# Overflowing pairs of experts: nested branches with one common Else, and gate and up loads issued ahead of down loads

## The reference

```python
def hierarchical_moe(h, wg_r, bg_r, we_r, be_r, w_gate, w_up, w_down):
    hf = h.reshape(n, d_)                                   # 512 x 1024
    gsel = jnp.argmax(group_logits, axis=-1)                # one group of 8 experts per token
    top_val, top_idx = lax.top_k(in_group, TOP_K_IN_GROUP)  # two experts in it
    gates = gp * jax.nn.softmax(top_val, axis=-1)
    ...
    def expert_block(args):
        tok, e = args
        xb = h_pad[tok]
        hid = jax.nn.silu(xb @ w_gate[e]) * (xb @ w_up[e])  # 1024 -> 256
        return hid @ w_down[e]                              # 256 -> 1024
    ...
    y = jnp.zeros((n + 1, d_), h.dtype).at[buf_tok].add(out)[:n]
```

## Time and profile before

| | us |
|---|---|
| runs of the kernel | 2876.44 median of 3 (2875.86 to 2879.05) |
| the profiled execution | 2879.38, its span 2877.6 |
| PE busy | 2341.8 (81%) |
| PE weight loads busy | 1718.4 (60%) |
| DVE busy | 1195.9 (42%) |
| ACT busy | 855.9 (30%) |
| POOL busy | 190.1 (7%) |
| DMA | 377.27 MB, mean 131 GB/s |
| granted TensorE clock, mean | 0.856 |

### The profile page before, as it was taken

The page is one execution under the profiler, slowest core; times in us unless marked ns, Lnnn a source line. Parts: engine busy times, 40 slices in busy tenths (PEclk is TensorE's granted clock), DMA queues, the critical chain, the costliest instruction groups (busy, mean ns, idle before and its releaser), DMA issues. The chain is left out here.

```text
span 2877.6 us, 32597 instructions
## 1 busy us (share of the span) xinstructions
PE 2341.8 (81%) x13804; PEld 1718.4 (60%) x13804; DVE 1195.9 (42%) x1868; ACT 855.9 (30%) x1270; POOL 190.1 (7%) x190
## 2 busy tenths in 40 slices
PE   7889999958953677679999979866698688887874
PEld 5768888837722676368888768555696533333331
DVE  3346664374168444556664344344424411111112
ACT  4324442274241222434442243553103210110000
POOL 0000000000014000000000000000310011111100
PEclk9889999979976677789999989955857699998997
DMA  4112222222200100112222213300103379999986
GB/s 180 59 59 88 90 101 91 85 88 88 73 0 9 15 13 13 74 59 93 98 98 90 105 64 112 95 0 8 17 1 144 124 320 419 418 418 413 402 347 271
DMA packets 106598, 377.27 MB, mean 131 GB/s; under 512 B 54960, under 2 KB 55744, under 8 KB 67536
## 3 DMA queue, kind: packets, MB, share of 16 engines
q1 hardware_dynamic: 94064, 363.55, 33.5%
q0 software_dynamic: 12384, 11.58, 1.4%
HBM read 375.31 MB, written 27.53 MB: 140 GB/s over the span
## 5 line engine op out<-in xcount | busy, mean ns | idle before, releaser
L579 PE MATMUL ps<-xh,wh 128*128 128x512 f32 x1384 | 552.7, 399 | 86.2 <-DVE wl L546 35.0
L580 PE MATMUL ps<-xl,wh 128*128 128x512 f32 x1384 | 548.5, 396 | 0.0
L581 PE MATMUL ps<-xh,wl 128*128 128x512 f32 x1384 | 547.5, 396 | 0.0
L546 DVE TENSOR_TENSOR wl<-raw,wh 128x2048 fp32r<-128x2048 f32 (+2 forms) x127 | 264.5, 2082 | 326.7 <-ACT wh L540 326.7
L579 PEld LDWEIGHTS ps<-xh,wh 128*128 128x128 f32 x1384 | 266.0, 192 | 160.4 <-issue 55.3
L581 PEld LDWEIGHTS ps<-xh,wl 128*128 128x128 f32 x1384 | 265.7, 192 | 56.5
L580 PEld LDWEIGHTS ps<-xl,wh 128*128 128x128 f32 x1384 | 266.4, 193 | 54.7
L2955 PE MATMUL ps<-egu,XT 128*64 128x512 f32 x1088 | 245.9, 605 | 28.6 <-DMA egu<-e_up 27.7
L540 ACT ACTIVATE wh<-raw 128x2048 fp32r<-128x2048 f32 (+2 forms) x127 | 220.4, 1735 | 82.4 <-PE ps L864 69.2
L3007 PE MATMUL ps<-ed,HID 128*64 128x512 f32 x544 | 151.3, 706 | 63.4 <-DMA ed<-e_down 61.6
L2955 PEld LDWEIGHTS ps<-egu,XT 128*64 128x64 f32 x1088 | 83.5, 139 | 166.6 <-issue 142.4
(11 more groups left out here) (460 smaller groups left out, 3487.1 us busy)
## 6 DMA issues: line engine op xcount, KB each, us to landing
egu<-e_gate SPq DMA_DIRECT2D x68, 1024.0 KB, 14.8
egu<-e_up SPq DMA_DIRECT2D x68, 1024.0 KB, 25.1
ed<-e_down SPq DMA_DIRECT2D x68, 1024.0 KB, 24.7
raw<-up SPq DMA_DIRECT2D x44, 1024.0 KB, 4.8
raw<-down SPq DMA_DIRECT2D x32, 704.0 KB, 4.0
raw<-rwkv_rkv SPq DMA_DIRECT2D x12, 1024.0 KB, 4.8
raw<-in_dn SPq DMA_DIRECT2D x8, 1024.0 KB, 4.8
raw<-sgu_u SPq DMA_DIRECT2D x4, 1024.0 KB, 8.3
```

What stands on the lines that cost most here:

```text
L546: e.tensor_tensor(K.WL[s][:, 0:n], K.RAW[r][:, 0:n], K.WH[s][:, 0:n].bitcast(F32), SUB).then_inc(*K.w_low.mark(i))
L579: e.matmul(o, h[:, q, k], x_high[:, k], start=k == 0, stop=False)
L580: e.matmul(o, h[:, q, k], x_low[:, k], start=False, stop=False)
L581: last = e.matmul(o, l[:, q, k], x_high[:, k], start=False, stop=k == KT - 1)
```

## The change

The eight branches, which stood one behind another, stand inside each other: the body of level q contains the If of level q+1, so an engine leaves all further levels with one branch. The Else of level q adds at once what all levels from q to 39 would have added, after waits for its engine's own semaphores; the waits for all engines in the Else of SP and POOL are gone. On SP a level issues gate and up of its own pair, and then the down loads of the pair before (`downs(q - 1)`); the down loads of the last executed pair stand in the Else that ends the levels (`last(q - 1, True)`), and SP then waits there until they have landed. The bodies of PE, ACT, DVE and POOL are as before.

```diff
         e.dma_start(K.EGU[slot][:, half], src).then_inc(*K.egu_in[slot].landing(i, half))
 
 
-def load_down(K, e, i, index=None):
+def load_down(K, e, i, index=None, counted=True):
+
     slot = i % 4
     w = K.A["e_down"]
     if i < 64:
@@ -2877,7 +2878,8 @@
         src = None if index is None else w[bass.ds(index, 1)].rearrange("a (p j) n -> p (a j) n", p=128)
     if i >= 4:
         e.wait_ge(*K.expert_sum("down", (i - 4) // 2))
-    e.dma_start(K.ED[slot][:, :, :], src).then_inc(*K.ed_in[slot].landing(i))
+    e.dma_start(K.ED[slot][:, :, :], src).then_inc(*(K.ed_in[slot].landing(i) if counted else (K.ed_in[slot].sem, 16)))
+    return K.ed_in[slot]
...
-def over_the_count(K, e, engine, q, body):
-
-
-    K.board.point(engine, "over", q)
+def over_the_counts(K, e, engine, body, last=None):
+
+
+
     if not e.real:
-        K.skipped[engine, q] = owed(K, engine, body)
+        for q in range(32, NP):
+            K.board.point(engine, "over", q)
+            K.skipped[engine, q] = owed(K, engine, lambda: body(q))
+        if last:
+            K.skipped[engine, NP] = owed(K, engine, lambda: last(NP - 1))
         return
-    met = dict(e.met)
-    with e.real.If(K.regs[engine] > 2 * (q - 32)):
-        body()
-    e.met = met
-    with e.real.Else():
-        for s, first, by in K.skipped[engine, q]:
-            e.real.wait_ge(s.sem, first)
-        if engine in ("POOL", "SP"):
-            for t in K.board.all_at("over", q):
-                e.real.wait_ge(*t)
-        for s, first, by in K.skipped[engine, q]:
-            e.real.sem_inc(s.sem, by)
+
+    def level(q):
+        met = dict(e.met)
+        with e.real.If(K.regs[engine] > 2 * (q - 32)):
+            body(q)
+            if q + 1 < NP:
+                level(q + 1)
+            elif last:
+                last(q)
+        e.met = dict(met)
+        with e.real.Else():
+            added = {}
+            for p in range(q, NP + 1):
+                for s, first, by in K.skipped.get((engine, p), ()):
+                    n = added.setdefault(s, [first, 0])
+                    n[1] += by
+            if last and q > 32:
+                for s in last(q - 1, True):
+                    added[s][0] += 16
+                    added[s][1] -= 16
+            for s, (first, by) in added.items():
+                e.real.wait_ge(s.sem, first)
+            for s, (first, by) in added.items():
+                if by:
+                    e.real.sem_inc(s.sem, by)
+        e.met = met
+
+    level(32)
...
-    for q in range(32, NP):
-        def body():
-            for i in (2 * q, 2 * q + 1):
-                if e.real:
-                    K.index[i] = e.real.value_load(K.OVI[0:1, i - 64:i - 63], min_val=0, max_val=63)
-                load_gate_up(K, e, i, K.index.get(i))
-            for i in (2 * q, 2 * q + 1):
-                load_down(K, e, i, K.index.get(i))
-        over_the_count(K, e, "SP", q, body)
+
+    def downs(q, again=False):
+        return [load_down(K, e, i, K.index.get(i), not again) for i in (2 * q, 2 * q + 1)]
+
+    def body(q):
+        for i in (2 * q, 2 * q + 1):
+            if e.real:
+                K.index[i] = e.real.value_load(K.OVI[0:1, i - 64:i - 63], min_val=0, max_val=63)
+            load_gate_up(K, e, i, K.index.get(i))
+        if q > 32:
+            downs(q - 1)
+    over_the_counts(K, e, "SP", body, downs)
...
-    for q in range(32, NP):
-        def body():
-            turn_pe(K, e, q)
-            gate_up_pe(K, e, q)
-            turn_hidden_pe(K, e, q)
-            down_pe(K, e, q)
-        over_the_count(K, e, "PE", q, body)
+
+    def body(q):
+        turn_pe(K, e, q)
+        gate_up_pe(K, e, q)
+        turn_hidden_pe(K, e, q)
+        down_pe(K, e, q)
+    over_the_counts(K, e, "PE", body)
```

More of the change, by code:

```diff
@@ L3143, in experts_act, with body @@
     overflow_count(K, e, "ACT")
[L3144 to L3149, removed]
+    def body(q):
+        turn_act(K, e, q)
+        gate_up_act(K, e, q)
+        down_act(K, e, q)
+    over_the_counts(K, e, "ACT", body)
     K.board.point("ACT", "mixed")
@@ L3166, in experts_dve, with body @@
     overflow_count(K, e, "DVE")
[L3167 to L3173, removed]
+    def body(q):
+        turn_dve(K, e, q)
+        gate_up_dve(K, e, q)
+        turn_hidden_dve(K, e, q)
+        down_dve(K, e, q)
+    over_the_counts(K, e, "DVE", body)
     K.board.point("DVE", "mixed")
@@ L3197, in experts_pool, with body @@
     overflow_count(K, e, "POOL")
[L3198 to L3207, removed]
+    def body(q):
+        gather(K, e, q + 1)
+        if q + 1 < NP:
+            e.wait_ge(*K.xg_more(q + 1))
+            e.memset(K.MARK[:, 0, q:q + 1], 0.0).then_inc(*K.pool_expert.mark("gathered", q + 1))
+        scatter(K, e, q, True)
+        e.wait_ge(*K.otok_more(q))
+        e.memset(K.MARK[:, 1, q:q + 1], 0.0).then_inc(*K.pool_expert.mark("scattered", q))
+    over_the_counts(K, e, "POOL", body)
     K.board.point("POOL", "mixed")
```

## The result

The changed kernel takes 2882.1 us (median of 20 runs, 2880.16 to 2883.62), the kernel before 2877.68 (20 runs, 2875.63 to 2880.14): a ratio of 1.0015, 95% interval 1.0008 to 1.0022, or 4.4 us more (by the interval 2.3 to 6.3). That is inside the 0.2% that I had called no change, on the slow side and clear of nothing, and as large as the predicted sum of 4.4.

A forecast was written before the change was run, and what follows sets the result against it. Full, in-order DMA queues bound the expert stage, then a 4.02 us tail before `OT`. Terms 5.7 + 2.0 - 3.3 = +4.4 us on a median of 2876.44 gave 2880.8 us, range 2876.0 to 2884.3.

The forecast's parts named there:

- Down loads late: Pair 32's down loads, queued behind four gate and up loads, make PE start its down product at 2836.9: cost 5.7 us.
- Rival 2: Pair 32's down loads aren't late; PE starts that down product at 2831.23 as before: -3.3 us, 2873.1, chance 0.10.
- Clock: PE idles 6.2 us before pair 32's down product, so its clock is lowered there: cost 2.0 us, between 0 and 3.65.
- Rival 3: PE's clock after its idle time isn't lowered, or recovers at once: +2.4 us, 2878.8, chance 0.12.
- Block 67's up comes too early to be of use: Block 67's up lands 5 us earlier, but gate and up of pair 33 can't use it: gain 0.
- Common Else: At the end, `OT` goes out 0.7 us behind the last MEMSET instead of 4.02: gain 3.3 us.
- lower bound of 2.0: Least gain at the kernel's end, if SP's last waits take as long again as the rest: 2.0 us.
- Far branches: PE's single jump past six pairs takes 2.9 us after its last product, hidden with 2.0 us to spare.
- Rival 1: POOL's far jump over six levels stalls on the path as PE's did, costing 2.9: +7.3 us, 2883.7, chance 0.13.
- SP's repeated down loads: Pair 33's down loads now stand in SP's Else, which SP reaches before 2812.27: cost 0.
- Sum: All terms after the 32 fixed pairs together: +4.4 us, to 2880.8 us, 0.15% slower.
- anything ahead of 2800 us: Sign of being wrong: the change should leave everything before about 2800 us as it was.

The follow-up runs named there:

- last experiment: Six matmuls added in PE's idle time ahead of gate and up of pair 32, against the kernel with common Else and old load order: 2874.23 us, ratio 0.9987.
- third experiment: Changed kernel plus seven matmuls whose result nothing reads, in PE's idle time before the down product of pair 32: 2880.08 us, ratio 1.0006.
- the second: Changed kernel, but down loads of pair 32 moved behind two loads instead of four (between gate and up of blocks 66 and 67): 2875.85 us, ratio 0.9993.
- fourth experiment: Changed kernel with gate and up of blocks 64 and 65 also put ahead of the down loads of pair 31: 2879.88 us, ratio 1.0005.

## Why the prediction was right, step by step

- **Down loads late (5.7 us): right.** By the rows PE's wait grew from 0.52 to 6.31, 5.8. It started at 2835.91, a microsecond before the forecast, behind a gate and up that itself had started 1.6 earlier. The run with the old order has no such wait, that with half the move 0.45 of it: the loads land in the order of issue, and the slack is what decides. Rival 2 falls with that.
- **Clock (2.0 us, taken from a nearby row): 2.4** (6.03 against 3.65), shown by the run in which PE is kept busy. Rival 3 falls. Gate and up of pair 32 took 0.48 more than before too (9.60, 9.12), in a lowered clock as before; I had no term for it, and it is not the change's, since the run with the old order has 9.43.
- **Block 67's up comes too early to be of use: right**, gate and up of pair 33 wait for `XT`. (Four loads of 2.8 behind 2820.04 give 2831.2, not the 2831.8 that I wrote; nothing hung on it.) The last experiment shows the other side of it: in the old order that load is one step from being the limit.
- **Common Else (3.3 us): 3.84**, 4.02 down to 0.18. I had left 0.3 for SP's last waits; they were nearly all done before POOL's addition. What I had put at nothing is the 0.3 us that the way from the last product to the MEMSET got longer, so 3.5 in all. My lower bound of 2.0 does not come out of my own numbers (4.02 less twice 0.7 is 2.6).
- **Far branches: right that they are hidden, wrong on where PE's stands.** I charged 2.9 from the end of PE's last product on. It took 3.766, but it overlapped with the last down product, so its addition stood at 2856.8, 5 us ahead of POOL's. POOL's single jump took no longer than 0.050. Rival 1 falls. By the Trainium skill (Runtime: NRT & Kernel Launch, "Instruction fetch mechanics") a branch beyond the pages held waits for a fetch; PE's 3.766 agrees in kind, and POOL's jump over six levels, which passes far less code, shows no stall.
- **SP's repeated down loads: right.** The down loads of pairs 32 and 33 are all out by 2815.25 (2808.36 + 6.89), and the last down product waits 0.52 for DVE and for no load.
- **Sum.** The three forecast terms measure 5.8 + 2.4 - 3.8 = 4.4; with the 0.3 us ahead of the MEMSET and 0.1 less in the turning of pair 33 it is 8.56 - 0.48 - 3.52 = 4.6 by the rows, 4.4 by the medians. The mechanism was right in each part, but that the sum met the tenth is luck: the clock was put 0.4 too low and the gain up to 0.5 too low, and the two cancel; and the interval of the ratio is 2 us wide to each side. The profiled spans differ by 3.7 (2881.3, 2877.6): in the changed kernel's profile block 65's up landed sooner after its issue, and PE waited 4.37 for it instead of 6.73. That isn't the change's doing: the same order of loads shows 6.50 in the third experiment's trace.
- **Did anything ahead of 2800 us move?** I had named that as a sign of being wrong, and in the profiled execution something did. The down product of pair 29, first in the kernel before, then in the changed one:

```profile
2792.12 3.65 PE L3007 MATMUL ps<-ed,HID 128*64 128x512 f32 x16 [2.24 <-DMA ed<-e_down]
```

```profile
2791.28 6.16 PE L3009 MATMUL ps<-ed,HID 128*64 128x512 f32 x16 [3.82 <-DMA ed<-e_down]
```

SP's loads up to there are the same in both kernels, and the third experiment, whose loads are the changed kernel's, has 2.13 and 3.65. So the order of loads does not force it; the traces of the second and fourth experiment show it too (3.85 and 6.46, 3.05 and 5.34), and what brings it about stays open. The 8.56 and the 3.5 are counted from behind it.

What I had wrong in the main came after the prediction: the belief that a load moved ahead at level 32 would fill idle DMA engines.

## What to carry to other kernels

In a queue that is full and served in order, moving a load ahead is moving others back: ask first which of them has less slack than the loads moved past it take (here 4.4 us against four loads of 2.8 each), and whether the one moved ahead is waited for at all. A change of two parts should be timed in its parts: this one hid 3.9 us of gain behind 8.3 of loss, and the version with the Else alone beats both kernels. Before filling a gap in the DMA share, check that no load in flight lands after the gap.

## What the runs showed of the hardware

- The 16 DMA engines do not finish together: with a share of 0.23 (3.7 engines' worth) for 5 us, a load issued 12 us before was still to land 7 us later, and of its 16 increments the last four came 4 to 14 us behind the twelfth. Which engines lag, and why, stays open. The Trainium skill (DMA: Bandwidth & Descriptors, "Latency and other measured facts") says that engines 7 and 15 are usually slower; no row here names an engine, and a share of 0.23 speaks for more than two.
- PE's sequencer went through the far branch while the array was still working: 3.766 us that cost nothing.
- An idle time of PE of 6.3 us cost 2.4 us more in the product behind it, one of 0.97 still 1.7 (5.35 against 3.65). The slow gate and up product before it is not needed for that: in the fourth experiment gate and up took 7.09, and behind a wait of 1.05 the down product still took 5.35. Nor does the length of the last wait decide by itself: in the kernel before a down product behind 2.24 us of idle time took 3.65, and in the last experiment gate and up behind 2.95 took 7.09. What does decide stays open.
